# Prompt masks and forget sums as single-pass products, and the group norms' sums of squares inside the next weight chunk

## What is computed

```python
def fox_block(q, cq, qpos, k, v, ck_t, kpos):
    s = jnp.einsum('bqhd,bkhd->bhqk', q, k).astype(jnp.float32) * (HEAD_DIM ** -0.5)
    s = s + cq.astype(jnp.float32).transpose(0, 2, 1)[..., None] - ck_t[:, :, None, :]
    s = jnp.where((kpos[None, :] <= qpos[:, None])[None, None], s, -jnp.inf)
    p = jax.nn.softmax(s, axis=-1)
    return jnp.einsum('bhqk,bkhd->bqhd', p.astype(v.dtype), v)
...
    y_cat = jnp.stack([y_pool, y_lru, y_fox.reshape(b, t, G), y_sb.reshape(b, t, G)], axis=2)
    y_cat = rms_norm(y_cat, out_g.reshape(N_GROUPS, G)).reshape(b, t, D_MIX)
```

## Time and profile before

| | us |
|---|---|
| median of 3 runs | 2624.44 (2619.4 to 2627.09) |
| the profiled execution | 2623.07 |
| its span | 2621.4 |
| PE busy | 2534.5 (97% of the span) |
| DVE busy | 1325.9 (51%) |
| ACT busy | 914.9 (35%) |
| POOL busy | 204.2 (8%) |

### The profile page before, as it was taken

How to read it: one execution, slowest core, us unless ns; L and a number is a source line. 1 busy time by engine, 2 the same in 40 slices (tenths; PEclk the granted TensorE clock), 3 DMA queues, 4 the chain that set the end, 5 groups by cost and what they waited for, 6 DMA issues and landing times.

```text
span 2621.4 us, 43516 instructions
## 1 busy us (share of the span) xinstructions
PE 2534.5 (97%) x16842; PEld 2331.3 (89%) x16842; DVE 1325.9 (51%) x1860; ACT 914.9 (35%) x1577; POOL 204.2 (8%) x320
## 2 busy tenths in 40 slices
PE   7999999999999979999999999999999999999998
PEld 7999998755565559999999999999999999999998
DVE  6345455334343456454554554554554554554555
ACT  5244455423232344332332332332332332332333
POOL 2060000133333300000000000000000000000000
PEclk9999999999999979999999999999999999999999
DMA  6293232699999932222222222222222222222222
GB/s 205 85 67 106 95 98 82 249 335 369 355 367 361 331 151 88 90 83 95 81 85 93 81 91 87 81 86 92 81 91 87 81 85 93 81 91 87 89 89 101
DMA packets 115362, 356.75 MB, mean 136 GB/s; under 512 B 30937, under 2 KB 39130, under 8 KB 90978
## 3 DMA queue, kind: packets, MB, share of 16 engines
q1 hardware_dynamic: 94402, 286.34, 33.1%
q0 software_dynamic: 20768, 67.65, 7.1%
HBM read 340.20 MB, written 13.74 MB: 135 GB/s over the span
## 4 chain that ended last, share of the span: by engine, by line
PE 85%; DVE 5%; issue 3%; ACT 3%; DMA 2%; SPq 2%; ACTq 0%; DVEq 0%
PE bank L419 48%; PE bank L424 24%; PE bank L1803 3%; PE bank L1745 2%; PE bank L1782 2%; DMA w_raw<-weights 1%; ACT w_hi L406 1%; DVE sum_tmp L488 1%; PE bank L1689 1%; PE bank L1684 1%; SPq L618 1%; SPq L622 1%; PE bank L1605 1%; ACT sum_tmp L482 1%; PE bank L1718 1%
## 5 line engine op out<-in xcount | busy, mean ns | idle before, releaser
L419 PE MATMUL bank<-x_act,w_hi 128*128 128x364 f32 (+1 forms) x4848 | 1061.9, 329 | 25.4 <-DVE x_act L500 13.1
L419 PEld LDWEIGHTS bank<-x_act,w_hi 128*128 128x128 f32 x4848 | 774.0, 189 | 28.0 <-issue 13.6
L419 PE MATMUL bank<-hid,w_hi 128*128 128x364 f32 (+1 forms) x3456 | 728.8, 329 | 18.6 <-DVE sum_tmp L488 17.6
L424 PE MATMUL bank<-x_act,w_lo 128*128 128x272 f32 x3232 | 650.5, 287 | 1.4 <-issue 1.4
L488 DVE TENSOR_TENSOR sum_tmp<-sum_tmp,bank 128x544 f32<-128x544 f32 x336 | 241.9, 720 | 723.2 <-ACT sum_tmp L482 723.2
L419 PEld LDWEIGHTS bank<-hid,w_hi 128*128 128x128 f32 x3456 | 555.0, 188 | 28.7 <-DVE sum_tmp L488 25.9
L424 PEld LDWEIGHTS bank<-x_act,w_lo 128*128 128x128 f32 x3232 | 563.1, 189 | 3.5 <-issue 2.2
L481 ACT ACTIVATE sum_tmp<-bank 128x184 f32<-128x184 f32 x336 | 108.7, 323 | 1021.9 <-PE bank L419 1021.8
L424 PE MATMUL bank<-hid,w_lo 128*128 128x272 f32 x2304 | 429.1, 287 | 0.0
L410 DVE TENSOR_TENSOR w_lo<-w_raw,w_hi 128x2048 fp32r<-128x2048 f32 x173 | 396.9, 2294 | 52.1 <-ACT w_hi L406 46.9
L424 PEld LDWEIGHTS bank<-hid,w_lo 128*128 128x128 f32 x2304 | 379.1, 188 | 0.0
(11 more groups left out here) (225 smaller groups left out, 1555.1 us busy)
## 6 DMA issues: line engine op xcount, KB each, us to landing
w_raw<-weights SPq DMA_DIRECT2D x173, 1024.0 KB, 4.8
k_ring<-fox_k SPq DMA_DIRECT2D x128, 256.0 KB, 5.1
v_ring<-fox_v POOLq DMA_DIRECT2D x128, 256.0 KB, 5.1
k_ring<-sb_k SPq DMA_DIRECT2D x128, 256.0 KB, 5.2
v_ring<-sb_v POOLq DMA_DIRECT2D x128, 256.0 KB, 5.4
wo<-w_early SPq DMA_DIRECT2D x16, 512.0 KB, 6.3
x_in<-xT SPq DMA_DIRECT2D x4, 1088.0 KB, 10.8
kv_out<-proj SPq DMA_DIRECT2D x4, 1088.0 KB, 9.8
```

The lines of the kernel that those rows point to most:

```text
L419: ins = nc.tensor.matmul(bank[:, base + b, 0:n], hi, row[:, t:t + n], start=begin, stop=end)
L424: ins = nc.tensor.matmul(bank[:, base + b, 0:HALF], lo, row[:, t:t + HALF], start=False, stop=False)
```

## The change

Three edits. First, the mask products and the forget-sum product of `scores` take fp32r operands. The two masks become one tensor `diagonal` of 129 columns, of which the two masks are windows that lie one column apart. The forget sum is split in two fp32r parts, the high part in rows 0 to 7 and the rest in rows 64 to 71 of a `c_prompt` with 72 rows, the rows between being zero; a selector `two_rows` adds both in one product over 72 rows. ScalarE makes rounded copies of the constants in chunk 4 and the high part between two `v_store`s; VectorE makes the low part behind the query tiles; GpSimd clears `c_prompt`. Second, the sums of squares of the early group norms are issued inside the chunk after (31 and 33) ahead of its sixth channel tile, by a new argument `first` of `multiply_tile`, in place of behind chunks 30 and 32. Third, in those chunks `between` comes ahead of the twelfth channel tile, not the ninth.

```diff
 N_PARAM = _at
 
 
-_K = [("ident", P), ("ones", P), ("same_head", P), ("fox_mask", P), ("sb_mask", P),
-      ("pool_rec", GT * POOL_MAX), ("before", P), ("minus_one", 1)]
+_K = [("ident", P), ("ones", P), ("same_head", P), ("diagonal", P + 1),
+      ("two_rows", HEADS), ("pool_rec", GT * POOL_MAX), ("before", P), ("minus_one", 1)]
 CONST, _at = {}, 0
 for _name, _n in _K:
     CONST[_name] = _at
...
     top = r.take("top", [1, P])
     r.end += 4096
     decay = r.take("decay", [P, 2, PAGE * 4 + NEW])
+    ident_r = r.take("ident_r", [P, P], F32R)
+    diagonal_r = r.take("diagonal_r", [P, P + 1], F32R)
+    two_rows_r = r.take("two_rows_r", [P, HEADS], F32R)
     r = Region(A_RAW, A_PROJ)
     w_raw = [r.take(f"w_raw{i}", [P, CHUNK]) for i in range(2)]
     w_hi, w_lo = [None, None], [None, None]
...
     k_ring = r.take("k_ring", [P, 4, 4, PAIRS, PAGE])
     dconst = r.take("dconst", [P, N_DCONST])
     pc = r.take("pc", [P, SEQ])
-    c_prompt = r.take("c_prompt", [HEADS, SEQ])
+    c_prompt = r.take("c_prompt", [HEAD_DIM + HEADS, SEQ], F32R)
     xh = [r.take(f"xh{i}", [P, HALF]) for i in range(X_SLOTS)]
     r = Region(A_ACT, A_END)
     v_ring = r.take("v_ring", [P, V_SLOTS, 4, D_GROUP])
...
     lf_gather = sem("lf_gather")
     lf_ln = sem("lf_ln")
     new_lf = sem("new_lf")
+    const_round = sem("const_round")
+    c_cleared = sem("c_cleared")
+    c_sum = sem("c_sum")
+    c_high = sem("c_high")
     c_ready = sem("c_ready")
     head_sq = sem("head_sq")
     head_rs = sem("head_rs")
...
     def y_row(k):
         return hid[:, k // GT, k % GT]
 
-    def multiply_tile(pe, c0, n, per=0, i=0, step=0, split=None, between=None):
+    def multiply_tile(pe, c0, n, per=0, i=0, step=0, split=None, between=None, first=None):
 
         pe.wait_ge(w_low, c0 + 1 + step * i)
         hi = w_hi[c0 % 2][:].rearrange("p (k n) -> p k n", k=KT)
...
         for k in range(KT):
             if split is not None:
                 pe.wait_ge(a_low, split + k + 1)
-            if between and k == KT // 2:
+            if first and k == 5:
+                first()
+            if between and k == (KT - 5 if first else KT // 2):
                 between()
             ins = products(tile_of(n), hi[:, k], lo[:, k], x_act[:, k], k == 0, k == KT - 1)
             if k % 4 == 3:
...
         end_stage(pool, 1)
 
 
+        nc.gpsimd.memset(c_prompt[:].bitcast(F32), 0.0).then_inc(c_cleared, 1)
         for x in range(2):
             own.then(nc.gpsimd.memset(q_pad[x][:], 0.0))
         own.wait()
...
                 softplus_lam()
             if c == 2:
                 forget_log()
+            if c == 4:
+                act.wait_ge(consts_in, 16)
+                f(ident_r[:], ident, ACT.Copy)
+                f(diagonal_r[:], cc("diagonal", 0, P + 1), ACT.Copy)
+                f(two_rows_r[:], cc("two_rows", 0, HEADS), ACT.Copy).then_inc(const_round, 1)
             if step == 1:
                 gate_exps(g)
             if step == 2:
...
 
         for n in range(10):
             v_store(n)
+            if n == 4:
+                act.wait_ge(c_cleared, 1)
+                act.wait_ge(c_sum, 1)
+                f(c_prompt[0:HEADS], pc[0:HEADS], ACT.Copy).then_inc(c_high, 1)
         act.wait_ge(kv_stored, 16 * 3)
 
         def prompt_logs(i):
...
 
 
         dve.wait_ge(new_lf, 1)
-        v.tensor_tensor_scan(c_prompt[:], ones[0:HEADS, 0:1].to_broadcast([HEADS, SEQ]), logit[:, 0:SEQ], 0.0,
-                             ALU.mult, ALU.subtract).then_inc(c_ready, 1)
+        v.tensor_tensor_scan(pc[0:HEADS], ones[0:HEADS, 0:1].to_broadcast([HEADS, SEQ]), logit[:, 0:SEQ], 0.0,
+                             ALU.mult, ALU.subtract).then_inc(c_sum, 1)
         dve.wait_ge(head_norm, 8)
         dve.wait_ge(q_scaled, 1)
         dve.wait_ge(q_cleared, 1)
...
                     r0 = 8 * a + DEC_SEQ * h
                     v.tensor_copy(q_pad[x][o:o + HEAD_DIM, :, a, r0:r0 + DEC_SEQ], src).then_inc(q_padded, 1)
             v.tensor_copy(k_new[x][:], proj[:, (FK, SK)[x], :, SEQ:]).then_inc(q_padded, 1)
+        dve.wait_ge(c_sum, 1)
+        dve.wait_ge(c_high, 1)
+        v.tensor_tensor(c_prompt[HEAD_DIM:], pc[0:HEADS], c_prompt[0:HEADS].bitcast(F32), ALU.subtract).then_inc(c_ready, 1)
 
 
         dve.wait_ge(kv_stored, 16 * 3)
...
                 if c >= HEAD_AT:
                     head_sums(c - HEAD_AT)
 
-            multiply_tile(pe, c, c, split=0 if c == 0 else None, between=between)
+            def group_sums():
+                p = EARLY_AT.index(c - 1)
+                pe.wait_ge(y_sq, p + 1)
+                pe.wait_ge(head_rs, c - HEAD_AT)
+                for h in range(2):
+                    ins = mm(spare[:, h], ones, y_sum[:, h * HALF:h * HALF + HALF], start=True, stop=True)
+                ins.then_inc(y_mm, 1)
+
+            multiply_tile(pe, c, c, split=0 if c == 0 else None, between=between,
+                          first=group_sums if c - 1 in EARLY_AT else None)
             if c == 1:
                 pe.wait_ge(x_folds, 5)
                 sum_channels(pe, x_sq[:, 0], 0)
...
                    ).then_inc(decay_carry, 1)
             if step == 0:
                 decay_gate(g)
-            if c in EARLY_AT:
-                pe.wait_ge(y_sq, EARLY_AT.index(c) + 1)
-                pe.wait_ge(head_rs, c - HEAD_AT + 1)
-                for h in range(2):
-                    ins = mm(spare[:, h], ones, y_sum[:, h * HALF:h * HALF + HALF], start=True, stop=True)
-                ins.then_inc(y_mm, 1)
         pe.wait_ge(strips, 4 * C_OUT)
         end_stage(pe, 1)
 
...
 
 
         pe.wait_ge(signs_in, 16)
+        pe.wait_ge(const_round, 1)
         pe.wait_ge(v_stored, 10)
         pe.wait_ge(head_norm, 8)
         pe.wait_ge(q_scaled, 1)
...
             s = [bank[:, x, 0:n] for x in range(2)]
             if i >= 1:
                 pe.wait_ge(f_exp, i)
-            mm(s[0], ident[0:HEADS, h:h + 1].to_broadcast([HEADS, P]), c_prompt[:, 0:n], start=True, stop=False)
+
+            mm(s[0], two_rows_r[0:HEAD_DIM + HEADS, h:h + 1].to_broadcast([HEAD_DIM + HEADS, P]), c_prompt[:, 0:n],
+               start=True, stop=False)
             if i >= 1:
                 pe.wait_ge(s_diff, i)
             for x in range(2):
...
                 mm(s[x], proj[rows, (FQ, SQ)[x], h // 2, P * q:P * q + P], proj[rows, (FK, SK)[x], h // 2, 0:n],
                    start=(x == 1), stop=False)
             for x in range(2):
-                mm(s[x][:, P * q:n], ident, cc(("fox_mask", "sb_mask")[x], 0, P), start=False, stop=True
+                mm(s[x][:, P * q:n], ident_r[:], diagonal_r[:, x:x + P], start=False, stop=True
                    ).then_inc((f_score, s_score)[x], 1)
 
         def turn(k, x):
...
     put("ident", (i == j).astype(np.float32))
     put("ones", np.ones((P, P), np.float32))
     put("same_head", (i // HEAD_DIM == j // HEAD_DIM).astype(np.float32))
-    put("fox_mask", np.where(j <= i, 0, MASKED).astype(np.float32))
-    put("sb_mask", np.where(j < i, 0, MASKED).astype(np.float32))
+    row, key = np.indices((P, P + 1))
+    put("diagonal", np.where(key <= row, 0, MASKED).astype(np.float32))
     _, g, t = np.indices((P, GT, POOL_MAX))
     put("pool_rec", (1.0 / np.minimum(2 ** (g + 1), t + 1)).astype(np.float32).reshape(P, -1))
+    row, h = np.indices((P, HEADS))
+    put("two_rows", (row % HEAD_DIM == h).astype(np.float32))
     put("minus_one", np.full((P, 1), -1, np.float32))
     d = np.zeros((P, N_DCONST), np.float32)
 
```

## The result

The changed kernel takes 2633.07 us (median of 20 runs, 2625.14 to 2638.41), the kernel before 2620.85 us beside it (20 runs, 2615.37 to 2627.09). The ratio is 1.004, with a 95% interval of 1.0031 to 1.005: **slower** by 10.5 us by the ratio and 12.2 us by the medians, where 2605 us had been forecast, and outside the range. The profiled execution took 2633.63 us, 10.6 more than that of before.

A forecast was written before the change was run, and what follows sets the result against it. TensorE, busy for 97% of the span, was the bound, with key-page DMA nearly full in attention. Group sums 8.9 plus attention 10.5 less seam 0.3 made 19.1 us saved: median 2605 us, range 2597 to 2616.

The forecast's parts named there:

- The group sums: Projection stage: issuing the early norms' sums inside the next chunk removes two TensorE stalls, saving 8.9 us (6.5 to 9).
- The seam: Between projection and attention stages: added clearing, copies and subtraction cost 0.3 us (0 to 0.6).
- Long turns: Attention turns with units of 384 and 512 keys: 27.5 us becomes 26.4, with VectorE then holding TensorE some 0.6 us.
- the MLP stage after it is not touched: MLP stage, after attention: taken as unaffected by the change, with no term in the sum.
- Short turns: Attention turns with units of 128 and 256 keys: held by the key loop, gaining 0.3 us seven times, 2 us.
- Stage 2: Attention stage, about 500 to 932 us: forecast to gain 10.5 us, bounds 3 and 18.
- floor: Attention key loop of issues, last landing and 32 products: no turn shorter than 24.8 to 25.0 us.
- the clock falls: Rival, 5%: waits over 1 us in short turns slow TensorE to 1.2 GHz, adding 1.7 us each; total 2628.
- The rule on HBM: Attention stage: HBM's limit of about 358 GB/s would keep turns at 26.4 us or more; the prediction let it pass.
- saturation rival in its hard form: Attention transfers saturate at the 358 GB/s limit: total 2616 us, 5 of the 20% given to saturation.
- mask pair: Attention units: two fewer mask records at 0.11 us each save 0.22 us in each of 32 units, 7.0 us.
- forget sum: Attention units: a single-pass product costs 0.06 us per 128 columns plus 0.1 fixed, saving 15 us (12 to 17).

The follow-up runs named there:

- attention part alone: Masks and forget sums as in the changed kernel, group sums as in the kernel before, plus 192 filler instructions: 2631.37 us, ratio 1.0035.
- The best version: The changed kernel with SyncE's page lookups moved ahead of its wait and 64 filler instructions between the late norms: 2603.89 us, ratio 0.9933.
- values later: The changed kernel with 192 filler instructions at start and late norms, and value pages held until the turn's key pages landed: 2646.56 us, ratio 1.0094.

## Why the prediction was wrong

**The group sums**: right. 8.9 us in the profile, 8.2 (medians) or 9.7 us (ratio) in the run of that part alone, and TensorE is held up nowhere. **The seam**: right, too; from stage 1's last product to stage 2's first there are 9.8 us before and 9.6 after. The new copy on ScalarE takes its 0.5 us without moving the last store. **Long turns**: right, 26.23 us against 26.4, with VectorE ahead of the fourth unit as told (0.57 us of wait, forecast 0.6).

**The step that cost most is one half-sentence: "the MLP stage after it is not touched".** The sum has no term for that stage, and it became 16.0 us longer. None of its lines is edited, but its code moved. I counted the 96 removed records only as time and not as length of a program that the engine fetches. This costs 16.0 us in the profiles, 11 us by the medians between the changed kernel and the same with 64 instructions more, and 13.4 us in the kernel before with 64 more. The price has two parts: the six waits themselves, 6.5 us, and slower products, behind four of the six. That position matters, and modulo 256, is shown by five placements (0, +256 and -128: none; +64 and -192: six waits). That it is a block that arrives late is shown by the instruction queue: one packet more for each jump, and TensorE goes on 1.2 to 1.5 us after it has landed. The rule of the Trainium skill named above was there to be read when the prediction was made. It stood in no rival. Yet without this loss the time would have been 2621.7 us (64 instructions more), still outside the range, so the next step counts too.

**Short turns: the second step that failed.** Stage 2 was to give 10.5 us and took 4.3 in this pair of profiles. The prediction took a floor of 24.8 to 25.0 us "with a landing of about 3.8 us" and gave the case "the clock falls" 5%. It happened in three of the six short turns behind the first, and once more in the last turn, by the place and price given there: 1.7 us of slower products inside the key loop. Its point of decision, waits of over 1 us, does not hold, since the length of the last wait alone does not decide. In the changed kernel 1.53 to 1.75 us did no harm. The timeline of the attention part alone has both kinds the other way round:

```profile
635.31 3.64 PE L1770 MATMUL bank<-k_ring,q_pad 128*32 128x512 f32 x32 [2.63 <-DMA k_ring<-sb_k]
...
871.73 5.34 PE L1770 MATMUL bank<-k_ring,q_pad 128*32 128x512 f32 x32 [1.27 <-DMA k_ring<-fox_k]
```

What was wrong besides was the size of the waits, 1.1 to 1.4 us in the text and 1.5 to 4.3 us in the trace. The landing is not a constant. For the last page of a short turn it was 4.1 us on average and became 5.2; for that of a long turn it was 4.8 and became 4.1. So the whole did not grow, and the floor, built from one observed turn, held a term that changes when the turns shift against the other transfers. What exactly lengthens it in the short turns stays open, and no run isolated the fall of the clock.

**The rule on HBM.** The limit of about 358 GB/s for one core (the Trainium skill, "DMA: Bandwidth & Descriptors", section Specifications) did not bind here. The best version moves 379 GB/s in the window above. The prediction's 9.47 MB a turn in its mean of 25.5 us (357.28 us for 14) make 371 GB/s. The mean was not a ceiling either, so the saturation rival in its hard form falls. Its signs did show: landings over 5 us in the short turns, and turns of 26.5 us on average, over its 26.0. But over these turns the rate was 355 GB/s, where it had been 359 before, and earlier issues raised it to 370: the rate was not at its ceiling.

**Sizes.** A mask pair takes 0.28 us from start to start (715.10 to 715.38 below) instead of 0.55: 0.27 us a unit, 8.6 us in all, forecast 7.0. That is 0.14 us a record both ways, where the prediction took 0.11 from the transposes. The forget sum is off more. The timeline of the changed kernel, a unit of 128 keys and one of 384:

```profile
714.33 0.42 PE L1711 MATMUL bank<-c_prompt,two_rows_r 72*128 72x128 f32 x1
714.68 0.49 PE L1717 MATMUL bank<-proj 64*128 64x128 f32 x4
715.10 0.44 PE L1720 MATMUL bank<-diagonal_r,ident_r 128*128 128x128 f32 x2
715.38 0.63 PE L1731 MATMUL bank<-const,pf 128*128 128x128 f32 x4
...
793.96 0.54 PE L1711 MATMUL bank<-c_prompt,two_rows_r 72*128 72x384 f32 x1
794.43 0.92 PE L1717 MATMUL bank<-proj 64*128 64x384 f32 x4
```

From its start to the next product it takes 0.35 us at 128 columns and 0.47 at 384: 0.06 us per 128 columns as forecast, but 0.29 us fixed, where 0.1 was taken. It saves 9.4 us (0.06, 0.21, 0.37 and, by extension, 0.53 a unit), under the lower bound of 12; the upper bound of 17 was a slip as well, by its own terms 18.4. Whether the 72 rows or something else makes the fixed part is not tested. Together 18 us came off TensorE instead of 22. With the issue loop and the jump out of the way 7 us of them reached the end by the medians.

## What to carry to other kernels

When a change alters the number of instructions ahead of a hardware loop, look at the first products behind each jump back; an "issue" wait there that was not before is the place of the code, and a few satisfied waits ahead of the loop can move it. The number of instruction packets on the page tells the same. Work taken from an engine that shares its bound with a DMA issue loop turned into waits here, and where the clock fell behind them the gain became a loss: shorten the issue loop first, by doing lookups ahead of the wait. Do not build a floor from one landing time: here it moved by 1.1 us in the short turns and by 0.7 us the other way in the long ones.

## What the hardware showed that was not expected

- The same loop, instruction for instruction, takes 1489.6 us instead of 1472.0 from another place in the program: six gaps of 1.2 to 1.7 us behind six jumps, slower products behind most of them, and 151 packets of instructions instead of 145.
- The length of a wait does not tell whether the clock falls. Waits for keys of 2.39, 2.63 and 2.80 us kept the 32 products at 3.64 us, the 2.4 GHz level (the version with lookups and group sums alone, the attention part alone, values later); waits of 1.27 and 1.53 us were followed by 5.34 us, the 1.2 GHz level (attention part alone, values later). Waits of 1.80 and 1.46 us with 1.6 us of products between them were followed by a granted clock of 0.66, waits of 1.79 and 1.13 us by 1.00.
- A single-pass record of 72 rows holds TensorE for 0.29 us beyond its columns, a pair of 128 rows for 0.28 us in all.
- Sixteen issues with a page number looked up between them take 17.2 us; with lookups done before, 9 to 12 us, while each issue alone shows 0.34 us in the median. The pages then land later after their issue (7.9 and 9.3 us in the median, 4.4 and 5.3 in the changed kernel), and still the turn is shorter.
